# Four edits to the order of work in a two-layer encoder kernel: convolution before solve, merge by four banks, first groups by pairs, residual stored in halves

## What is computed

```python
for l in range(DEPTH):
    x = x + 0.5 * rms_norm(swiglu(rms_norm(x, ...), ffn1_w_in[l], ffn1_w_out[l]), ...)
    u = rms_norm(x, mix_pre_norm[l])
    (dq, dk, dv, dz, db, da, sq, sk, sv, gate_a, gate_b) = split(u @ mix_w_in[l])
    y_a = deltanet_branch(dq, dk, dv, dz, db, da, ...)   # convolution of 4 taps, silu, gated delta rule
    y_b = swa_sink_branch(sq, sk, sv, ...)               # rope, window attention with sinks
    merged = sigmoid(gate_a) * (y_a @ w_branch_a[l]) + sigmoid(gate_b) * (y_b @ w_branch_b[l])
    x = x + rms_norm(merged @ mix_w_out[l], mix_post_norm[l])
    x = x + 0.5 * rms_norm(swiglu(rms_norm(x, ...), ffn2_w_in[l], ffn2_w_out[l]), ...)
```

## Time and profile before

| | |
|---|---|
| median of 3 runs | 2298.76 us (2297.09 to 2298.92) |
| the profiled execution | 2298.68 us, its span 2296.9 us |
| TensorE busy | 2249.0 us, 98% |
| VectorE busy | 1007.6 us, 44% |
| ScalarE busy | 820.0 us, 36% |
| GpSimd busy | 74.8 us, 3% |
| mean granted TensorE clock | 0.992 |
| moved by DMA | 215 MB, 94 GB/s |

### The profile page before, as it was taken

How to read it: one execution, slowest core, us unless ns; L and a number is a source line. 1 busy time by engine, 2 the same in 40 slices (tenths; PEclk the granted TensorE clock), 3 DMA queues, 4 the chain that set the end, 5 groups by cost and what they waited for, 6 DMA issues and landing times.

```text
span 2296.9 us, 29581 instructions
## 1 busy us (share of the span) xinstructions
PE 2249.0 (98%) x11656; PEld 1880.6 (82%) x11656; DVE 1007.6 (44%) x1424; ACT 820.0 (36%) x1403; POOL 74.8 (3%) x104
## 2 busy tenths in 40 slices
PE   7999999999999999999999999999999999999998
PEld 6888888778887888888888888887788878888887
DVE  3434324683435543432253433247824355443423
ACT  5323214533543432322252322156335325332211
POOL 0000000001000100000000000010000001000000
PEclk9999999999999999999999999999999999999999
DMA  4232332321122332222232222332212233323222
GB/s 161 92 101 93 99 96 79 119 74 56 56 74 92 129 110 93 99 95 98 83 111 94 98 98 94 101 112 82 74 47 65 74 116 112 103 93 99 101 93 82
DMA packets 67417, 215.15 MB, mean 94 GB/s; under 512 B 15216, under 2 KB 15984, under 8 KB 66800
## 3 DMA queue, kind: packets, MB, share of 16 engines
q1 hardware_dynamic: 65584, 201.10, 26.9%
q0 software_dynamic: 1728, 12.58, 1.5%
HBM read 206.84 MB, written 6.82 MB: 93 GB/s over the span
## 4 chain that ended last, share of the span: by engine, by line
PE 90%; DVE 5%; ACT 2%; DMA 1%; issue 1%; SPq 0%; DVEq 0%; ACTq 0%
PE ps L504 20%; PE ps L506 20%; PE ps L505 20%; PE ps L548 8%; PE ps L549 8%; PE ps L550 8%; DMA raw<-in_wstream_dram 1%; DVE tmp L1443 1%; DVE wlo L1263 1%; PE ps L516 1%; PE ps L721 1%; DVE ulo L1303 1%; ACT uhi L954 1%; PE ps L782 1%; PE ps L675 1%
## 5 line engine op out<-in xcount | busy, mean ns | idle before, releaser
L1263 DVE TENSOR_TENSOR wlo<-raw,whi 128x1024 fp32r<-128x1024 f32 (+1 forms) x376 | 456.0, 1214 | 922.2 <-ACT whi L904 911.2
L504 PE MATMUL ps<-uhi,whi 128*128 128x512 f32 (+1 forms) x2208 | 832.6, 377 | 20.0 <-DVE ulo L1303 9.0
L505 PE MATMUL ps<-ulo,whi 128*128 128x512 f32 (+1 forms) x2208 | 822.7, 373 | 0.0
L506 PE MATMUL ps<-uhi,wlo 128*128 128x512 f32 (+1 forms) x2208 | 822.6, 373 | 0.0
L904 ACT ACTIVATE whi<-raw 128x1024 fp32r<-128x1024 f32 (+1 forms) x372 | 389.8, 1049 | 922.7 <-PE ps L506 542.2
L504 PEld LDWEIGHTS ps<-uhi,whi 128*128 128x128 f32 x2208 | 419.1, 190 | 99.0 <-issue 18.9
L506 PEld LDWEIGHTS ps<-uhi,wlo 128*128 128x128 f32 x2208 | 419.0, 190 | 72.4
L505 PEld LDWEIGHTS ps<-ulo,whi 128*128 128x128 f32 x2208 | 419.4, 190 | 71.3 <-issue 1.0
L548 PE MATMUL ps<-whi,hhi 128*128 128x512 f32 x704 | 274.4, 390 | 0.0
L550 PE MATMUL ps<-whi,hlo 128*128 128x512 f32 x704 | 274.0, 389 | 0.0
L549 PE MATMUL ps<-wlo,hhi 128*128 128x512 f32 x704 | 273.9, 389 | 0.0
(11 more groups left out here) (218 smaller groups left out, 1599.0 us busy)
## 6 DMA issues: line engine op xcount, KB each, us to landing
raw<-in_wstream_dram SPq DMA_DIRECT2D x368, 512.0 KB, 3.5
x_home<-x POOLq DMA_DIRECT2D x2, 2048.0 KB, 7.9
x<-x_home POOLq DMA_DIRECT2D x2, 2048.0 KB, 8.4
gain<-in_gp_dram POOLq DMA_DIRECT2D x6, 512.0 KB, 6.2
x<-in_x_dram SPq DMA_DIRECT2D x4, 512.0 KB, 8.3
raw<-in_wstream_dram SPq DMA_DIRECT2D x8, 256.0 KB, 3.1
out_dram<-x SPq DMA_DIRECT2D x8, 256.0 KB, 2.1
rcs<-in_rope_dram POOLq DMA_DIRECT2D x2, 512.0 KB, 10.6
```

The source lines that it names most:

```text
L504: pe.matmul(o, lh, bhi, start=first, stop=False)
L505: pe.matmul(o, lh, blo, start=False, stop=False)
L506: return pe.matmul(o, ll, bhi, start=False, stop=last)
L1263: dve.tensor_tensor(wlo[:, s, 0:cols], raw[:, s % RAWS, 0:cols], whi[:, s, 0:cols].bitcast(f32), ALU.subtract) \
```

## The change

It has four parts, and a fifth that belongs to the fourth.

1. In step list 14 the last convolution and silu 10 come before the solve.
2. The merge reads four banks into `tmp` 0 to 3 first, then does the four sums, then the four low parts.
3. In `first_group` the chunk s=0 goes by pairs of tiles (tiles 0 and 1 for both k, then 2 and 3); token tile 3 is turned in two halves inside s=3, not behind it.
4. The residual is stored in halves: the first at the mixer's start, the second behind chunk 4's steps when VectorE has made the decay's operand; silu 0 waits for the first, silu 8 for the second. The table for rope is loaded behind chunk 6's steps.

```diff
-    s[14] = [("solve",), ("conv", 11), ("silu", 10)]
+    s[14] = [("conv", 11), ("silu", 10), ("solve",)]
...
-            def turn_tile(L, st, t):
+            def turn_tile(L, st, t, halves=(0, 1)):
...
-                for half in range(2):
+                for half in halves:
...
-                        for i in range(2):
-                            k = 2 * s + i
-                            pe.wait_ge(u_lo.h, u_lo.at(L, u0 + k + 1))
-                            for m in range(4):
...
-                        if h == 0 and s >= 2:
-                            turn_tile(L, st, s)
+                        for pair in ((0, 1), (2, 3)) if s == 0 else (range(4),):
+                            for i in range(2):
+                                k = 2 * s + i
+                                pe.wait_ge(u_lo.h, u_lo.at(L, u0 + k + 1))
+                                for m in pair:
+                                    if h == 0 and k == 0:
+                                        pe.wait_ge(u_lo.h, u_lo.at(L, u0 + (3, 4, 7, 8)[m]))
+                                    last = mm3(bank(m, 2 * P * h, 2 * P), (c + s) % RING, i * 4 + m, uhi[:, k, cols], ulo[:, k, cols],
+                                               k == 0, k == KT - 1)
+                                    if h and i:
+                                        last.then_inc(gemm_done.h, 1)
+                                    if h == 0 and s == 3 and (i, m) in ((0, 3), (1, 1)):
+                                        turn_tile(L, st, 3, (i,))
+                        if h == 0 and s == 2:
+                            turn_tile(L, st, 2)
...
-                        act.activation(uhi[:, i, :], tmp[:, 4 + i % 2, :], ACT.Copy, scale=0.5).then_inc(mg_hi.h, 1)
+                        act.activation(uhi[:, i, :], tmp[:, i % 4, :], ACT.Copy, scale=0.5).then_inc(mg_hi.h, 1)
...
                     dve.wait_ge(g_in.h, g_in.at(L, 16 * (n + 1)))
+                    if n == 1:
+                        dve.wait_ge(mg_lo.h, mg_lo.at(L, 8))
...
-                            if i >= 2:
-                                dve.wait_ge(mg_lo.h, mg_lo.at(L, i - 1))
...
+                            if i == 4:
+                                dve.wait_ge(mg_lo.h, mg_lo.at(L, 4))
+                            dve.scalar_tensor_tensor(tmp[:, i % 4, :], gates[:, i, :], 1.0, bank(b), ALU.add, ALU.mult).then_inc(tile_read.h, 1)
+                            if i % 4 == 3:
+                                for q in range(i - 3, i + 1):
+                                    dve.wait_ge(tile_read.h, tile_read.at(L, TILE_M + 8 + q + 1))
+                                    dve.tensor_tensor(tmp[:, q % 4, :], tmp[:, q % 4, :], m1[q // 4][:, q % 4, :], ALU.add).then_inc(mg_done.h, 1)
+                                for q in range(i - 3, i + 1):
+                                    dve.wait_ge(mg_hi.h, mg_hi.at(L, q + 1))
+                                    dve.scalar_tensor_tensor(ulo[:, q, :], tmp[:, q % 4, :], 0.5, uhi[:, q, :].bitcast(f32), ALU.mult,
+                                                             ALU.subtract).then_inc(mg_lo.h, 1)
...
                             dve.wait_ge(x_out.h, x_out.at(L, 16))
+                        elif i == 8:
+                            dve.wait_ge(x_out2.h, x_out2.at(L, 16))
...
-                pool.dma_start(x_home, x[:, :, :]).then_inc(x_out.h, 16)
-                pool.dma_start(rcs[:, :, :], rope).then_inc(rope_in.h, 16)
+                pool.dma_start(x_home[:, 0:2, :], x[:, 0:2, :]).then_inc(x_out.h, 16)
...
+                    if j == 4:
+                        pool.wait_ge(gs_done.h, gs_done.at(L, 1))
+                        pool.dma_start(x_home[:, 2:4, :], x[:, 2:4, :]).then_inc(x_out2.h, 16)
+                    if j == 6:
+                        pool.wait_ge(misc_out[6].h, misc_out[6].at(L, USE[("decay", 0), 6] + 1))
+                        pool.dma_start(rcs[:, :, :], rope).then_inc(rope_in.h, 16)
```

## The result

| | kernel before | changed kernel |
|---|---|---|
| median | 2298.07 us (2293.01 to 2298.92, 6 runs) | 2279.79 us (2275.12 to 2283.65, 6 runs) |
| the profiled execution, its span | 2298.68 us, 2296.9 us | 2280.74 us, 2278.9 us |
| mean granted TensorE clock | 0.992 | 0.994 |

The ratio is 0.9925, 95% interval 0.9911 to 0.9939: 17.2 us of the kernel before (14.0 to 20.5), where 14.7 were forecast. 2279.79 lies inside the range of 2276 to 2291. The runs of the changed kernel spread over 8.5 us, and their mean granted clock goes with it: 2283.5 and 2283.7 us at 0.992, 2275.1 at 0.995. One execution can thus be some 4 us off without the kernel having changed, and the experiments are read from marks inside the traces first.

A forecast was written before the change was run, and what follows sets the result against it. TensorE, busy for 98% of the span, was taken as the bound, so only its waits could be won. Gains of 4.6 + 2.8 + 6.9 + 0.4 = 14.7 us off 2298.7 gave 2284.0 us, range 2276 to 2291.

The forecast's parts named there:

- First groups: First groups, pairs and tile 3 in halves: 0.6 us at each of five boundaries plus 1.6 at kernel start, 4.6 us.
- the start: The group at the kernel's start, where both ends count: 1.6 us gained, ends 0.7 and 2.2.
- The store: Mixer's start, residual in halves and rope later: TensorE's 2.5 us wait on cv and two restarts go, 2.8 us.
- The wait of ScalarE on raw: Near the mixer's start: such a wait was named as a sign that the prediction is wrong.
- The merge: Branch product and output stage, four banks read first: 6.0 us of TensorE waits and six restarts go, 6.9 us.
- The move: Last convolution before the solve: the 4.31 us stall goes, but VectorE's chain to Z decides; 0.4 us, ends -3 and +5.
- The two waits of VectorE for M+19 and M+20: VectorE, behind the solve, waits for splits of mixer weight chunks 19 and 20: 0.65 and 1.0 us.
- TensorE's new waits: Four smaller stalls between 504 and 517.5 us replace the 4.3 us one: 3.1, 1.3, 1.1 and 1.1 us.
- The slow clock rival: Around Z: the stall comes back as half clock, 2290.8 us, or 2287 if it straddles Z; chance 0.22.

The follow-up runs named there:

- e1_pairs: Kernel before with only the first weight chunk of each first group by pairs of tiles, tile 3 turned behind its chunk as before: 2294.94 us, ratio 0.9986.
- a3_store: Kernel before with only the residual stored in halves and rope's load moved later: 2293.14 us, ratio 0.9983.
- a4_first: Kernel before with only the first groups changed (pairs of tiles and tile 3 turned in halves): 2288.83 us, ratio 0.9964.
- e2_halves: Kernel before with only tile 3 turned in halves inside its last weight chunk, order of the first chunk kept: 2291.46 us, ratio 0.9973.
- a2_merge: Kernel before with only the merge by four banks: 2289.75 us, ratio 0.9969.
- a1_conv: Kernel before with only the last convolution and silu 10 moved ahead of the solve: 2297.43 us, ratio 1.0.
- c1_noconv: Changed kernel with the last convolution back behind the solve, the other three edits kept: 2281.07 us, ratio 0.9929.
- b3_both: Changed kernel with loads of mixer chunks 19 and 20 issued early, and masks and products of q and k moved behind Z: 2278.52 us.
- b1_loads: Changed kernel with the loads of mixer chunks 19 and 20 issued ahead of SyncE's wait for the solved block and its DMAs: 2278.11 us, ratio 0.9913.
- g3_poolnoconv: Changed kernel with loads of chunks 19 and 20 early, two mask operations on GpSimd, last convolution back behind the solve: 2286.45 us, ratio 0.9952.

## Why the prediction was right, point by point

- **First groups, 4.6 us.** At the five boundaries 0.6 to 0.75 us each, 3.3 in all, where 3.0 were summed. The first half transposes of tile 3 started at 393.36 in the changed kernel, 0.8 us behind the start of ScalarE's scaling, 0.7 in the sum. Missing in the sum are the six waits of 0.33 us on the second chunk's split, which take most of what the pairs won. The pairs alone bring 0.1 us a boundary (e1_pairs). The term that was mis-sized is the start: 1.6 taken, ends 0.7 to 2.2, and 3.5 us found. Of these about 1.2 go with a half clock that the trace of before happened to have; the edit's part, 0.9 to 2.3, fits the term. The 1.2 us are luck.
- **The store, 2.8 us.** The two traces give 2.2 us at chunk 4 in layer 0 and 0.8 in layer 1, 3.0 in all; a3_store gives the same 3.0 in its trace and 3.9 in its runs. The load landed 6.5 us behind the issue of the store, inside the 4 to 8 of the prediction, and the store of 1 MB landed after 4.4 us, as it estimated (4.7 in a3_store). The wait of ScalarE on raw that it named as a sign of being wrong is there (3.00 us), but TensorE doesn't wait for it: as a sign it was badly chosen, since a load landing at 408 to 412 meant such a wait. What the prediction missed is that the first groups' edit also moves the issue of the store, worth 0.5 us in a4_first and 0.2 in e2_halves. This overlap is too small to explain that the parts measured alone sum to 0 + 7.1 + 3.9 + 8.3 = 19.3 us against 17.2 together; each of them is uncertain by some 2 to 3 us.
- **The merge, 6.9 us.** Measured 7.8 us in the trace of the changed kernel, 3.9 a layer, and the same in a2_merge. The mechanism is the one described. The extra 0.45 us a layer may be the price of resuming after a wait, which I put at 0.15 us each; no run separates it.
- **The move, 0.4 us.** Right in kind: 0.3 us in the traces, 0.1 in a1_conv's and 0.1 to 0.5 by c1_noconv, not 8. Counted from chunk 4, the inverse came 0.75 us earlier in layer 0 (0.6 predicted) and 0.5 later in layer 1 (0.2 predicted). Part of the loss in layer 1 is luck of the trace of before: a2_merge has the same code there, and its inverse comes 0.7 us later than in the kernel before. There VectorE waited 0.78 us at its first rope, which in layer 1 of before it didn't. The two waits of VectorE for M+19 and M+20 came as 0.35 and 1.40 us, predicted 0.65 and 1.0: the sum of 1.65 against 1.75. TensorE's new waits came as 2.86, 0.16, 1.15 and 0.75 us, predicted 3.1, 1.3, 1.1 and 1.1.
- **The slow clock rival.** It didn't happen in the change: behind Z the granted clock is 1.00 over 7 us in both layers, and no half clock comes until the stretch that was there before. It did in b3_both, where a wait of 3.24 us in front of the inverse was followed by a loss of 3.1 us.
- **The forecast of 2284.0** was 4.2 us too high. Of it 3.3 us are in the profiled execution: 1.9 at the start, of which some 1.2 are the half clock, 0.9 in the merge, 0.3 at the boundaries, 0.2 at the store, less 0.1 at the move. The other 0.9 us lie between that execution and the median.

b1_loads has the lowest median of all, 2278.11 against 2279.79 us. Its range lies inside that of the changed kernel, so that it beats it is likely from the table, with the inverse 1.6 us earlier in each layer, but not shown by its times.

## What to carry to other kernels

A wait of the busiest engine is worth the distance to the next thing that it needs. Add up the row of steps of the engine behind the wait up to that point, its waits for loads included, before pricing the edit: here 8.5 us of waits were worth 0.1 to 0.5. Look at what else hangs on an event that an edit makes earlier, as the store did here on the last rounding; and when a step is taken from ahead of a load, expect idle time unless the load is issued earlier too.

## What the runs showed of the hardware that I had not expected

- VectorE's three operations with both inputs in SBUF went from 2.31 to 6.34 us while GpSimd did two masks of 2.6 and 2.75 us. GpSimd's power just before them, on 128x16, left VectorE's 1.23 us operation on NN at 1.23.
- The same code at the kernel's start ran at half clock for most of 18 to 25 us in one trace, for half of that in another, and not in two. The lengths of the stretches 21 to 26 us behind the inverse differ likewise, and cost 3.4 to 8.4 us over a run.
- One wait of 3.24 us ahead of the inverse was followed by a granted 0.58 over 7.5 us; one of 2.97 us there, and waits of 1.15 and 0.75 us, were followed by 1.00. In g3_poolnoconv 2.57 us at chunk 16 were followed by 0.50 over 3.4 us. What decides between them no run here shows.
